# Modulation rows in four column groups, norm roots in PSUM, and the shift in ScalarE's rounding, in a two-block transformer kernel

## What is computed

```
# first block, per layer
h = rms_norm(x, norm_w);  proj = h @ w_in           # split into branches
y_a = differential attention;  y_c = causal convolution branch
y_d = gated delta rule (chunked, a recurrence over units of heads)
x = x + (g_a * y_a + g_c * y_c + g_d * y_d) @ w_out

# second block, per layer
mod   = silu(c)     @ w_mod + b_mod                 # 1024 x 6144, one row
mod_c = silu(c_ctx) @ w_mod + b_mod                 # the same weights, a second row
shift1, scale1, gate1, shift2, scale2, gate2 = split(mod, 6)      # mod_c likewise
h = rms_norm_2(x, norm) * (1 + scale) + shift       # before attention/hyena and before SwiGLU
x = x + gate1 * mix(h);   x = x + gate2 * swiglu(h')
# rms_norm(x) = x / sqrt(mean(x * x) + eps) * gain
```

## Time and profile before

| | us |
|---|---|
| median of 3 executions | 2917.5 (2914.85 to 2925.42) |
| the profiled execution, its own time | 2918.11 |
| its span in the profile | 2915.9 |
| PE busy, PEld busy | 2677.2 (92%), 2206.4 (76%) |
| DVE, ACT, POOL busy | 1365.7, 1329.8, 1492.4 |
| DMA, mean over the span | 119 GB/s |

### The profile page before, as it was taken

The page is one execution under the profiler, slowest core; times in us unless marked ns, Lnnn a source line. Parts: engine busy times, 40 slices in busy tenths (PEclk is TensorE's granted clock), DMA queues, the critical chain, the costliest instruction groups (busy, mean ns, idle before and its releaser), DMA issues.

```text
span 2915.9 us, 41912 instructions
## 1 busy us (share of the span) xinstructions
PE 2677.2 (92%) x16512; PEld 2206.4 (76%) x16512; DVE 1365.7 (47%) x2172; ACT 1329.8 (46%) x2166; POOL 1492.4 (51%) x857
## 2 busy tenths in 40 slices
PE   6978999999997899999979899998999988898997
PEld 6966877868796687776857676775788867788897
DVE  8986733323788583333446642215100126745214
ACT  5445944454444594345443331234223334444543
POOL 6843854338784485342643122464455554273880
PEclk9988999999998899999999999999999999999999
DMA  6522433334452333324431111223122222134454
GB/s 224 180 100 95 144 134 116 116 130 167 166 188 92 111 131 130 121 103 145 143 128 72 44 58 59 72 98 108 72 87 101 87 101 101 60 129 159 167 183 143
DMA packets 50552, 347.62 MB, mean 119 GB/s; under 512 B 5312, under 2 KB 8640, under 8 KB 8896
## 3 DMA queue, kind: packets, MB, share of 16 engines
q1 hardware_dynamic: 47840, 340.31, 32.6%
q10 hardware_dynamic: 2528, 4.72, 0.5%
HBM read 343.96 MB, written 1.05 MB: 118 GB/s over the span
## 4 chain that ended last, share of the span: by engine, by line
PE 75%; DVE 13%; ACT 7%; issue 3%; POOL 2%; DMA 1%; ACTq 0%; DVEq 0%; SPq 0%; POOLq 0%
PE pg L1653 18%; PE pg L1654 18%; PE pg L1655 18%; PE pg L1676 4%; DVE big L1261 2%; PE pg L1678 2%; PE ps L1899 2%; PE ps L1907 2%; DVE big L1258 1%; PE ps L1905 1%; POOL ring_lo L588 1%; PE ps L1792 1%; ACT ring_hi L693 1%; PE ps L2040 1%; PE ps L1773 1%
## 5 line engine op out<-in xcount | busy, mean ns | idle before, releaser
L588 POOL TENSOR_TENSOR ring_lo<-ring,ring_hi 128x1024 fp32r<-128x1024 f32 (+3 forms) x500 | 1180.0, 2371 | 940.2 <-ACT ring_hi L693 939.1
L1653 PE MATMUL pg<-HH,ring_hi 128*128 128x256 f32 (+1 forms) x3360 | 1070.9, 319 | 59.4 <-DVE HL L1182 40.1
L1654 PE MATMUL pg<-HH,ring_lo 128*128 128x256 f32 (+1 forms) x3360 | 1029.8, 306 | 0.0
L1655 PE MATMUL pg<-HL,ring_hi 128*128 128x256 f32 (+1 forms) x3104 | 957.1, 308 | 0.0
L1653 PEld LDWEIGHTS pg<-HH,ring_hi 128*128 128x128 f32 x3360 | 641.4, 191 | 130.2 <-issue 58.5
L1654 PEld LDWEIGHTS pg<-HH,ring_lo 128*128 128x128 f32 x3360 | 642.2, 191 | 41.0 <-issue 12.6
L1655 PEld LDWEIGHTS pg<-HL,ring_hi 128*128 128x128 f32 x3104 | 593.0, 191 | 30.9
L693 ACT ACTIVATE ring_hi<-ring 128x1024 fp32r<-128x1024 f32 (+6 forms) x564 | 555.8, 1001 | 30.6 <-issue 19.3
L703 ACT ACTIVATE take<-pg 128x256 f32<-128x256 f32 (+1 forms) x284 | 120.4, 424 | 491.7 <-PE pg L1655 441.9
L1655 PE MATMUL pg<-big_r,ring_hi 128*128 128x256 f32 (+1 forms) x864 | 276.2, 320 | 0.0
L1653 PE MATMUL pg<-big_r,ring_hi 128*128 128x256 f32 (+1 forms) x736 | 242.3, 329 | 13.7 <-issue 5.6
(11 more groups left out here) (286 smaller groups left out, 3553.8 us busy)
## 6 DMA issues: line engine op xcount, KB each, us to landing
ring<-in_w_stream_dram SPq DMA_DIRECT2D x320, 1024.0 KB, 4.8
hn<-in_consts_dram ACTq DMA_DIRECT2D x2, 1024.0 KB, 5.3
cst<-in_consts_dram SPq DMA_DIRECT2D x1, 1472.0 KB, 19.6
prm<-in_params_dram SPq DMA_DIRECT2D x1, 1110.0 KB, 7.4
X<-in_xT_dram SPq DMA_DIRECT2D x1, 1024.0 KB, 5.8
X<-in_ctxT_dram ACTq DMA_DIRECT2D x1, 1024.0 KB, 8.0
out_dram<-H ACTq DMA_DIRECT2D x1, 1024.0 KB, 5.1
cst<-in_consts_dram SPq DMA_DIRECT2D x1, 768.0 KB, 16.5
```

Source lines behind the costliest of these rows:

```text
L588: pool.tensor_tensor(ring_lo[:, slot, cols], ring[:, slot, cols], ring_hi[:, place * P:(place + n) * P].bitcast(F32), SUB).then_inc(sem(LO ...
L1653: first = pe.matmul(out, a[0], b[0], start=start, stop=False)
L1654: pe.matmul(out, a[1], b[0], start=False, stop=False)
L1655: return first, pe.matmul(out, a[0], b[1], start=False, stop=stop)
```

## The change

Three things are changed.

*Rows.* `sc` is widened to 32 columns for each c, two real ones and 30 zeros (in the place of a parameter used up by then; GpSimd writes the zeros, Silu moves to the first product's stage, and PE waits for both). Matmul c writes the 32 partitions `32 * (c % 4)` on of `pg`, so four matmuls use four groups of columns of the array, and the row is the sum of the four. ScalarE copies all 128 partitions, and the turn becomes four matmuls with `sel`, a 128x2 matrix of zeros and ones that adds the groups. A row has two parts of 4 matmuls instead of four of 2, in the delta dealing and around the norms.

*Root.* The sum of squares is added in PSUM (the last addition goes to `rstd`), and the root is `inverse_root` in PSUM: Ln, Exp. An Ln on one column ahead of the wait brings in its table. VectorE has no reciprocal and multiplies by the root out of PSUM. The ring's pieces due at the chunk before the root's go ahead of the root, the others no longer behind it at once.

*Shift.* In norms 3 to 6 VectorE multiplies by the root and by the scale, in halves of 256 tokens; ScalarE adds the shift and writes HH at once; VectorE makes HL as H + shift - HH, in halves.

```diff
     c["ones"] = np.ones((P, P))
+    c["sel"] = (i[:, None] % MOD_COLS == np.arange(2)[None, :]) * 1.0
...
-    return {"before": [("part", x) for x in rows[:1]] * 2, "after": rows, ...
+    return {"before": [("part", x) for x in rows[:1]], "after": rows, ...
...
-    return {"mod": 4, "modt": 1}.get(name, 2)
+    return {"modt": 1}.get(name, 2)
...
+        sc = PR("lam_qk", 0, KD * MOD_COLS).rearrange("p (a b) -> p a b", a=KD)
...
                 conv_gate(l)
+                if l == 0:
+                    pool.wait_ge(sem("lam_dots"), 1)
+                    pool.memset(sc[:, :, 2:MOD_COLS], 0.0).then_inc(sem("c_pad"), 1)
...
-                        act.activation(mod_rows[0:2, i % 2, :], ready(CHUNK[name, l, i])[0:2, :], ACT.Copy)...
+                        act.activation(mod_rows[:, i % 2, :], ready(CHUNK[name, l, i]), ACT.Copy)...
...
             def norm_root(i):
                 n = N_NORM[i]
+                if i in NORM_USER:
+                    ahead(CHUNK[NORM_USER[i]] - 1)
+                act.activation(warm[:, :], eps6, ACT.Ln)
                 act.wait_ge(sem("norm_ss"), i + 1)
-                act.activation(rstd[:, 0:n], ps[:, 0, 0:n], ACT.Sqrt, bias=eps6, scale=1.0 / D)\
-                    .then_inc(sem("norm_rms"), 1)
-                if i in NORM_USER:
-                    ahead(CHUNK[NORM_USER[i]])
+                inverse_root(ps[:, 0, 0:n], ps[:, 0, 0:n], eps6, 1.0 / D, "norm_rms")
...
-                for k in range(KD + 1):
+                for k in range(KD):
                     if k == KD // 2:
                         drain_fill(norm_mods(i, "after"))
-                    if k < KD:
-                        act.wait_ge(sem("normed"), KD * (i - 3) + k + 1)
-                        for s in range(n // T):
-                            ins = act.activation(H[:, k, s * T:(s + 1) * T], H[:, k, s * T:(s + 1) * T], ACT.Identity,
-                                                 bias=mod[:, l, 3 * which * KD + k, s:s + 1], scale=gains[:, which, k, s:s + 1])
-                        ins.then_inc(sem("h_whole"), 1)
-                    if k:
-                        high_part(i, k - 1)
+                    act.wait_ge(sem("normed"), KD * (i - 3) + k + 1)
+                    for s in range(n // T):
+                        ins = act.activation(HH[:, k, s * T:(s + 1) * T], H[:, k, s * T:(s + 1) * T], ACT.Identity,
+                                             bias=mod[:, l, 3 * which * KD + k, s:s + 1])
+                    ins.then_inc(sem("h_high"), 1)
...
             act.wait_ge(sem("first_tables"), 16)
+            ahead(0)
             norm_root(0)
-            ahead(0)
...
-                link(dve.reciprocal(rstd[:, 0:n], rstd[:, 0:n]))
                 for k in range(KD):
                     dve.scalar_tensor_tensor((H if dst is None else dst)[:, k, 0:n], X[:, k, 0:n], PR(gain, at + k),
-                                             rstd[:, 0:n], MUL, MUL)...
+                                             ps[:, 0, 0:n], MUL, MUL)...
...
-            def norm_over(i):
+            def norm_over(i, l, which):
...
                 norm_sum(i)
+                dve.wait_ge(sem("mod_done"), len(MOD_PARTS) * l + which + 1)
                 dve.wait_ge(sem("norm_rms"), i + 1)
-                link(dve.reciprocal(rstd[:, 0:n], rstd[:, 0:n]))
-                for k in range(KD + 3):
+                for k in range(KD + 2):
                     if k < KD:
-                        dve.tensor_tensor(H[:, k, 0:n], X[:, k, 0:n], rstd[:, 0:n], MUL).then_inc(sem("normed"), 1)
-                    if k >= 3:
-                        low_part(i, k - 3)
+                        for s in range(n // T):
+                            t = slice(s * T, (s + 1) * T)
+                            ins = dve.scalar_tensor_tensor(H[:, k, t], X[:, k, t], gains[:, which, k, s:s + 1], ps[:, 0, t], MUL, MUL)
+                        ins.then_inc(sem("normed"), 1)
+                    if k >= 2:
+                        moved_low(i, k - 2, l, which)
+
+            def moved_low(i, k, l, which):
+                dve.wait_ge(sem("h_high"), KD * SPLIT_NORMS.index(i) + k + 1)
+                for s in range(N_NORM[i] // T):
+                    t = slice(s * T, (s + 1) * T)
+                    ins = dve.scalar_tensor_tensor(HL[:, k, t], H[:, k, t], mod[:, l, 3 * which * KD + k, s:s + 1],
+                                                   HH[:, k, t].bitcast(F32), ADD, SUB)
+                ins.then_inc(sem("norm_h"), 1)
...
-                        ins = pe.matmul(pg[0:2, j % 4, :], sc[:, c, :], tile(4), start=c == 0, stop=c == k - 1)
+                        part = slice(c % MOD_TILES * MOD_COLS, (c % MOD_TILES + 1) * MOD_COLS)
+                        ins = pe.matmul(pg[part, j % 4, :], sc[:, c, :], tile(4), start=c < MOD_TILES, stop=c >= k - MOD_TILES)
...
-                    ins = pe.transpose(pg[:, j % 4, 2 * q:2 * q + 2], mod_rows[0:2, i % 2, q * P:(q + 1) * P], ident[0:2, 0:2])
+                    ins = pe.matmul(pg[:, j % 4, 2 * q:2 * q + 2], mod_rows[:, i % 2, q * P:(q + 1) * P], C("sel"), start=True, stop=True)
...
-                fill([("part", mods(l, "att")[0])] * 2)
+                fill([("part", mods(l, "att")[0])])
```

More of the change, by code:

```diff
@@ L31 @@
 LEAD = 24
+MOD_COLS = 32
+MOD_TILES = P // MOD_COLS
 AQ, AK, AV, AZ, GLU, CZ, DQ, DK, DV, DZ, DB, GATE = (
@@ L107 @@
 CONST_W = {"until": P, "later": P, "causal1": T, "levels": 7 * P, "rot1": P, "tab1": 2 * T,
-           "ident": P, "ones": P, "eps6": 1, "eps5": 1, "half_pi": 1, "lam_init": DEPTH, "inv1": 1,
+           "ident": P, "ones": P, "eps6": 1, "eps5": 1, "half_pi": 1, "lam_init": DEPTH, "inv1": 1, "sel": 2,
            "rot2": P, "cos2": T, "sin2": T, "zT": T, "dft_fwd": NT * N_FFT, "idft": 4 * T,
@@ L180, in norm_mods @@
     rows = [("mod", *x) for x in MOD_AT.get(("norm", i), [])]
-    return {"before": [("part", x) for x in rows[:1]] * 2, "after": rows, "turns": [("modt", *x[1:]) for x in rows]}[side]
+    return {"before": [("part", x) for x in rows[:1]], "after": rows, "turns": [("modt", *x[1:]) for x in rows]}[side]
 def att_fill(l):
@@ L407, in build @@
         gains = sb("gains", 2, KD, 2)
-        sc = sb("sc", KD, 2)
+        warm = sb("warm", 1)
         def cut(buf, at, *shape):
@@ L719, in drain_fill @@
                             act.wait_ge(sem("drained"), CHUNK[MOD_TURNS[k - 2]] + 1)
-                        act.activation(mod_rows[0:2, i % 2, :], ready(CHUNK[name, l, i])[0:2, :], ACT.Copy).then_inc(sem("drained"), 1)
+                        act.activation(mod_rows[:, i % 2, :], ready(CHUNK[name, l, i]), ACT.Copy).then_inc(sem("drained"), 1)
                     elif name == "modt":
@@ L905, in _ @@
             act.activation(WB_HI[:, :], PR("w_ba", 0, PARAM_W["w_ba"]), ACT.Copy).then_inc(sem("wb_high"), 1)
-            act.activation(sc[:, :, :], PR("c", 0, 2 * KD), ACT.Silu).then_inc(sem("silu_c"), 1)
             for l in range(DEPTH):
@@ L919, in _ @@
                         act.activation(lam[:, 0:4], lam[:, 0:4], ACT.Exp).then_inc(sem("lam_exp"), 1)
+                        act.activation(sc[:, :, 0:2], PR("c", 0, 2 * KD).rearrange("p (a b) -> p a b", a=KD), ACT.Silu)\
+                            .then_inc(sem("silu_c"), 1)
                 for j in range(16):
@@ L1167, in norm @@
                 dve.wait_ge(sem("norm_rms"), i + 1)
-                link(dve.reciprocal(rstd[:, 0:n], rstd[:, 0:n]))
                 for k in range(KD):
                     dve.scalar_tensor_tensor((H if dst is None else dst)[:, k, 0:n], X[:, k, 0:n], PR(gain, at + k),
-                                             rstd[:, 0:n], MUL, MUL).then_inc(sem("h_whole" if i in SPLIT_NORMS else "norm_h"), 1)
+                                             ps[:, 0, 0:n], MUL, MUL).then_inc(sem("h_whole" if i in SPLIT_NORMS else "norm_h"), 1)
                     if i in SPLIT_NORMS and k >= 2:
@@ L1191, in norm_sum @@
                 dve.wait_ge(sem("norm_sq"), KD * i + 2)
-                ins = dve.tensor_tensor(rstd[:, 0:n], H[:, 0, 0:n], H[:, 1, 0:n], ADD)
+                ins = dve.tensor_tensor(ps[:, 1, 0:n], H[:, 0, 0:n], H[:, 1, 0:n], ADD)
                 for k in range(2, KD):
@@ L1197, in norm_sum @@
                     dve.wait_ge(sem("norm_sq"), KD * i + k + 1)
[L1198 removed]
+                    ins = dve.tensor_tensor(ps[:, 1, 0:n] if k < KD - 1 else rstd[:, 0:n], ps[:, 1, 0:n], H[:, k, 0:n], ADD)
                 ins.then_inc(sem("norm_sum"), 1)
[L1201 removed]
+            def norm_over(i, l, which):
                 n = N_NORM[i]
                 norm_sum(i)
+                dve.wait_ge(sem("mod_done"), len(MOD_PARTS) * l + which + 1)
                 dve.wait_ge(sem("norm_rms"), i + 1)
[L1206 to L1207 removed]
+                for k in range(KD + 2):
                     if k < KD:
[L1209 to L1211 removed]
+                        for s in range(n // T):
[11 more added lines that the diff above has]
+                ins.then_inc(sem("norm_h"), 1)
```

(5 more changed lines are left out.)

1 line of the change is left out of this document (removed).

## The result

The changed kernel takes 2873.6 us (median of four executions, 2872.7 to 2877.1) against 2916.2 of the kernel before; the ratio is 0.9846, with a 95% interval of 0.9835 to 0.9858: 45 us less, 41 to 48 by the interval (the two medians lie 42.5 apart, the two profiled executions 45.4). 2850 was predicted, with a range of 2836 to 2888. The sign and the range hold, but the forecast's own neighbourhood, 2836 to 2862, is missed: of the 68 us forecast, 45 came.

What follows compares the result with a forecast made beforehand. TensorE was taken to bound the kernel, 75% of the chain of waits. From 2918.1 us, delta stages -37, gates -6.4, turns +5.3 and norms -30 sum to -68: 2850 us, range 2836 to 2888 (chance 0.8).

Steps and rivals of the forecast that it cites:

- rival 1: Modulation rows: groups overlap only in part, in program order, rows 4.4 us; total 2877 us; chance 0.15.
- rival 5: Norms bring little, -12 us instead of -30, with groups all at once; total 2868 us; chance 0.10.
- Overlap of the groups: Modulation rows: four column groups run all at once, a row falls from 7.03 to 1.8 us.
- rival 2: Modulation rows: groups give nothing, passes stay 0.43 us apart; total 2911 us; chance 0.10.
- rival 3: Modulation rows: each pass waits until the one before has left the array, row 9.7 us; total 2949; chance 0.05.
- rival 4: Norm roots: Ln and Exp stay in one table, 1.28 us shorter in 8 norms; total 2840 us; chance 0.02.
- Delta stages: Six rows a layer between the chain's steps: shorter rows give -18.5 us a layer, -37 in all.
- if the new clock falls: Stated sign of being wrong: TensorE's clock falls because PE is less busy around norms, 0.82 there before.
- Attention: Attention half rows and row "do": hidden, 0 us; turns there counted separately within the +5.3 us.
- Gates: One row a layer: bounded by PE's own input being ready, -6.4 us for two.
- Silu: Moved Silu on ScalarE, one more table load of 1.28 us, lies 200 us before its reader: 0.
- Norms: New root, PSUM operand free of contention and shift: -30 us in all, bounds -36 to -12.

Runs made afterwards that it cites:

- e3: Changed kernel with all eight matmuls of a row writing the same 32 columns' group, so nothing can overlap: 2924.8 us, ratio to before 1.0030.
- e11: Changed kernel with late Silu, fill of the delta stages dealt by length of the parts, and filled attention half rows: 2867.9 us, ratio 0.9823.
- e9: Changed kernel with zero-adding matmuls after those of the two attention half rows in each layer, filling PE's wait before the turn: 2873.5 us.
- e12: Changed kernel with the ring's pieces at a norm behind the root again, root still in PSUM: 2898.6 us, ratio 0.9931.
- e10: Changed kernel with the root written to SBUF instead of PSUM, so VectorE's multiplications have two SBUF inputs again: 2877.6 us, ratio 0.9853.

## Why the prediction was right, and where it was off

The total lies inside the range with some luck. The range was widened for rivals 1 and 5, and neither came true; what took 23 us off the forecast, waits and clock, had a term that was too small or none. By its total alone, 2873.6, rival 1 (2877) would have looked right; the row's length rules it out.

*Overlap of the groups.* Right, from the one row that was near in kind: 1.92 us a row against 1.8, and e3 shows that without groups nothing is left. Rivals 1, 2 and 3 are out by the row's length; e3 shows what rival 2 would have given, 2925 where I had 2911. Rival 4 is out: the changed kernel loads a table at each of the eight roots twice, once ahead of the wait, once between Ln and Exp.

*Delta stages*, the step that failed: -18.5 a layer against -8.8 and -10.5 (output included). In the first layer's stage the waits and the clock make up the miss of 9.5 us. First, the needs of the gaps were read in a kernel in which rows covered them. VectorE's chain behind the preparation has 4.2 us only when it runs clear of the low pieces; I had seen one gap that didn't, took off 3 us, and it happened in three of four. PE's work was to fall by 26 us (6 rows of 6.96 us against some 1.9, turns 0.6 more each) and the stage by 18.5, which leaves 7.5 us for more waiting; it was 12.6, the upper end of the idle time that I had said the profile would show. That is 5 us. Second, the clock: I had named it as what would make me wrong, "if the new clock falls", but only around the norms, and gave it nothing in the sum. PE's work fell by 21.7 us and not by 26; the other 4 are the clock, 0.96 for 0.99, as far as the sum tells: the stage has 7 us at half rate before and 20 after, and e11 shows the same stage 5.4 us shorter at 0.99.

*Attention*, set at no gain and no loss but the turn: +4.0 and +3.4. I had called the row hidden behind ScalarE. That is so, but the idle time that it leaves grew from 2.23 to 4.77 us, and behind it PE runs at half rate for longer. Of the 4.0 us this is some 2.2, by PE's starts from the second half row on; 1.5 are lost at once behind the gates, where the granted clock is 0.50 from 294.7 to 298 us and was 1.00 before. By the Trainium skill ("TensorE: Matmul & The Clock Gate", Part 1) PE falls to half its rate for want of recent work; e3 and e9 agree, with 1.12 and 1.11 us for two matmuls that take 2.06 after the longer wait.

*Gates*: -3.3 and -2.7 against -3.2 each; L1878 waits 1.00 us for L1327, the bound that I had taken.

*Silu*: costed at nothing because its reader is 200 us away. What I left out is who stands behind it on ScalarE: a high piece, then the low piece, then PE, 2.30 us idle, and then half rate. At the start this cost 2.8 us and hid norm 0's gain, which is there (last low part at 27.46, 27 was forecast).

*Norms*: right in size for each norm but the start. Norm 5, timeline of the changed kernel, to be read beside the earlier trace rows:

```profile
2362.26 0.64 ACT L754 ACTIVATE ps<-ps,cst 128x512 f32<-128x512 f32 x1
2362.93 1.28 ACT L756 ACT_TABLE_LOAD   x1
2364.22 0.58 ACT L756 ACTIVATE ps<-ps 128x512 f32<-128x512 f32 x1
2364.91 2.44 DVE L1215 SCALAR_TENSOR_TENSOR H<-X,gains,ps 128x256 f32<-128x256 f32 x6 [5.17 <-ACT ps L756]
...
2375.15 2.46 DVE L1225 SCALAR_TENSOR_TENSOR HL<-H,mod,HH 128x256 fp32r<-128x256 f32 x6
```

The root takes 2.6 us, VectorE 32 operations in 12.7, together 15.3 where I had 15.2 without the ring's two pieces. But the reason that I gave for the contended part is not what acts there: I put it on the PSUM operand. The operand does keep the multiplications short beside a low piece (e12), but in the changed kernel none stands beside one in norms 3 to 6, and by e10 it changes nothing there. What frees them, and the low parts too, is the order of the pieces, which I had only counted as a delay. The number came out by luck in this part, since in either story the multiplications run clear.

## What to carry to other kernels

When fill work in a list of gaps is made shorter, the needs of the gaps have to be read as they will be when the chain starts earlier: what ran one behind the other may then run side by side. Idle time left on TensorE behind a hidden operation isn't free even off the path, as the matmuls after it may run at the lower clock; fill it, but no longer than the wait. When TensorE's work is to be shortened, give the sum a term for the clock: here 24 of 107 us of saved work went that way. And an operation moved to another place on an engine can cost what is queued behind it, wherever its reader stands (here 2.8 us).

## What the runs showed of the hardware

Matmuls with 32 stationary columns each, on four column groups, run beside each other: 16 passes of fp32 over 512 columns in 1.92 us instead of 7.03, and the same with every pass doubled (3.9). VectorE's multiplications with one input in PSUM take 466 to 475 ns beside GpSimd's low pieces (18 in e12); with both inputs in SBUF they take up to 2.8 us on 512 columns before, and 2.5 us on 256 in e10. What I hadn't expected is the price of a few us of waiting: behind 4.77 us without work the turn takes 1.73 us instead of 1.05 and the next four matmuls 3.97 instead of 2.14, while behind 2.2 us none (e3) or only the later ones (before) run slower. Over the kernel the shorter rows go with 66 us more at half rate. And times won early need not reach the end: 2.8 us kept for 2400 us were lost within 50 us to a lower clock.
